# A trunk layer on one core: the columns of x for blocks 1 to 3 loaded from memory and normed there in place of transposes on TensorE, and value products that read two heads in turn

## The chip, the cores and the metric

The kernel runs on one core of a Trainium2 chip. Its time is the device time of one execution in microseconds; the figure quoted is the median of three runs. The engines that matter are PE (TensorE, matrix products), DVE (VectorE), ACT (ScalarE), POOL (GpSimd) and SP, which only issues transfers. Each runs its own instructions in order and waits on semaphores for the others.

## What is computed

One layer of a hybrid trunk over 2048 rows of 1024 columns, in float32:

```
h = _rmsnorm(x, norm1_g[layer])
proj = jnp.einsum('bsd,de->bse', h, w_in[layer])
(a_q, a_k, a_v, b_q, b_lat, i_q, i_k, i_w, gate_a, gate_b) = _split_cols(proj)
o_a = _mixer_a(...)          # sliding-window attention, 8 heads of 64, window 128, sinks
o_b = _mixer_b(...)          # indexer scores, the best 256 keys of a row, attention over them
merged = sigmoid(gate_a) * (o_a @ w_branch_a) + sigmoid(gate_b) * (o_b @ w_branch_b)
x = x + merged @ w_out
x = x + (silu(h2 @ w_ffn_gate) * (h2 @ w_ffn_up)) @ w_ffn_down     # h2 = _rmsnorm(x, norm2_g)
return _rmsnorm(x, norm_f_g)
```

Here `_rmsnorm(x, g)` is x times the inverse root of its row's mean square, times the gain g of each column. The change touches the first line (h, for three quarters of the rows) and the products of probabilities and values inside `_mixer_b`.

## The kernel before

**Tiling.** The rows are worked in four blocks of 512 (`NB`, `ROWS`). The 1024 columns lie as 8 groups of 128 (`KT`), called columns here: HT[:, k, :] holds 128 columns of h in the partitions and 512 rows along them, transposed. Products keep float32 accuracy by splitting each operand into a high part and a low remainder: `three` (L1065 to L1068) issues high x high, high x low and low x high for each column, so a job is 8 columns of three matmuls. `by_turns` makes the matmul read its 512 rows from two halves in turn, 1024 bytes apart; the result comes out in the natural order.

**Jobs.** A list (`JOBS`, L347) sets the order of the weight products: for each block b the projections iq 0 to 3 and ikw (indexer), lat (latent), and then the list `SECOND` (av, ak, aq 0 to 3, bq 0 to 3, gate 0 to 15; `s` counts in it, gate m is s = m + 10). After the projections of all four blocks follow attention, branches, output product and feed-forward, block by block. Between the columns of the SECOND jobs PE also does pieces of the indexer's scores (L1187, L1188); ACT takes their positive part (L1761) and DVE adds them up (L2337), with a MEMSET (L2342) that ends the scores of a block. In blocks 1 and 2 DVE also works at the search for the best keys of the block before (L2094 to L2131).

**Weights.** SP issues each job's weights (512 KB) into one of two buffers WRAW (L824), and behind them what `spill` adds for the job six before. POOL splits them: TENSOR_SCALAR makes WHI and TENSOR_TENSOR makes WLO (L1001, L1003), each twice per job, four columns at a time. The split of a job begins when PE has finished the job two before, since WHI and WLO have two buffers.

**The first norm and the transposes.** While block b is projected, the rows of block b + 1 lie in XN. ACT squares them at s = 11 and 12, DVE makes the mean at s = 13, ACT the root at s = 15, and DVE the inverse root SS and the scaled rows (L2056), four instructions at s = 16 to 19. PE then turns XN by multiplying with an identity (L1201): four transposes of 128x128 make one column of 128x512 in PSUM. Columns 0 to 3 of the next block are turned inside gate 15, the last job that reads the old HThi and HTlo, and columns 4 to 7 inside iq 0 of the next block. Of each turned column ACT makes HThi times the gain (L1806, `high_column`), and DVE makes HTlo as column times gain minus HThi (L2351), with the column read from PSUM. iq 0 waits for each column's HTlo (`h_split`). The gate's columns free HThi and HTlo (`h_used`).

**The value products.** In the second attention (kind "b") the transposed probabilities PThi and PTlo of two heads (128 queries each) are multiplied with the values VB: L1377 and L1379, 128x256 each, 1088 in all over the four blocks. ACT copies the sums out as XV (L1665).

## Time and profile before

| | |
|---|---|
| median of three runs | 3089.55 us (3085.45 to 3092.37) |
| profiled execution | 3089.96 us |
| its span, first to last instruction | 3087.5 us |
| PE busy | 3034.7 us (98%) |
| DVE, ACT, POOL busy | 58%, 46%, 66% |
| share of PE in the chain that ended last | 82% |
| mean granted clock of TensorE | 0.996 |

A row of a timeline gives start, duration, engine, line, instruction, output and inputs, and in brackets the idle time before it and what ended that. Matmuls overlap, so the time that one costs is the distance between two starts, not its duration. A row of a table by stretches gives, for each engine, its busy time and the number of instructions, and then the granted clock of TensorE.

### The profile page before, as it was taken

The page shows a single profiled execution, that of the slowest core. Times are in us where ns is not written, and L with a number is a line of the kernel's source. Part 1 is how long each engine was busy: PE and PEld are TensorE (multiplying, and loading weights), DVE is VectorE, ACT ScalarE, POOL GpSimd, SP SyncE. Part 2 cuts the span into 40 slices and gives each one's busy share as a digit, 9 for nine tenths or more (in the row PEclk, how much of TensorE's full clock was granted, in tenths as well). Part 3 has the DMA queues.
Part 4 walks back from the last instruction along what each step waited for, and adds up shares of the span by engine and source line. Part 5 has one row for each costly group of instructions (what it writes and reads, how often), then busy time and mean ns, then how long its engine had stood idle before and what let it go on. Part 6 is the DMA issues. An engine that isn't in the chain of part 4 may idle for free.

```text
span 3087.5 us, 44427 instructions
## 1 busy us (share of the span) xinstructions
PE 3034.7 (98%) x15678; PEld 2691.8 (87%) x15678; DVE 1805.0 (58%) x4109; ACT 1422.5 (46%) x2589; POOL 2025.0 (66%) x2201
## 2 busy tenths in 40 slices
PE   9999999999989999999999999999999999999998
PEld 8888888888888888898888888988888899888887
DVE  4336547637665555557766766967868689521111
ACT  3324545436463544347464534937655378320001
POOL 5666766665556677764777775376777922667777
PEclk9999999999999999999999999999999999999999
DMA  5766455355615333331533333163333510533333
GB/s 153 210 173 180 123 172 151 110 169 162 210 36 190 107 116 110 112 130 66 207 113 113 109 114 131 27 246 107 102 113 116 176 25 18 175 99 103 103 109 103
DMA packets 464204, 392.62 MB, mean 127 GB/s; under 512 B 29264, under 2 KB 394064, under 8 KB 463344
## 3 DMA queue, kind: packets, MB, share of 16 engines
q1 hardware_dynamic: 442544, 345.56, 37.2%
q10 hardware_dynamic: 21440, 44.22, 3.9%
q8 instruction: 126, 2.06, 0.3%
q14 instruction: 94, 0.77, 0.1%
HBM read 323.76 MB, written 62.81 MB: 125 GB/s over the span
## 4 chain that ended last, share of the span: by engine, by line
PE 82%; DVE 6%; ACT 4%; POOL 3%; issue 2%; DMA 2%; ACTq 0%; SPq 0%; DVEq 0%; POOLq 0%
PE BANK L1066 19%; PE BANK L1068 19%; PE BANK L1067 19%; PE BANK L1352 3%; PE LP L1066 3%; PE LP L1068 3%; PE LP L1067 3%; PE BANK L1377 2%; PE BANK L1379 2%; PE LP L1332 2%; PE LP L1333 2%; PE LP L1188 2%; PE LP L1187 2%; POOL WLO L1003 2%; DVE MASK L2094 1%
## 5 line engine op out<-in xcount | busy, mean ns | idle before, releaser
L1003 POOL TENSOR_TENSOR WLO<-WRAW,WHI 128x512 fp32r<-128x512 f32 x912 | 1209.3, 1326 | 76.0
L1001 POOL TENSOR_SCALAR WHI<-WRAW 128x512 fp32r<-128x512 f32 x912 | 633.3, 694 | 677.1 <-PE BANK L1068 521.8
L1066 PE MATMUL BANK<-H2hi,WHI 128*128 128x512 f32 x1376 | 524.9, 381 | 3.1 <-POOL WLO L1003 2.1
L1068 PE MATMUL BANK<-H2hi,WLO 128*128 128x512 f32 x1376 | 522.0, 379 | 0.0
L1067 PE MATMUL BANK<-H2lo,WHI 128*128 128x512 f32 x1376 | 521.9, 379 | 0.0
L1066 PE MATMUL BANK<-HThi,WHI 128*128 128x512 f32 (+1 forms) x1024 | 394.3, 385 | 1.2 <-DVE QS L2067 0.9
L1068 PE MATMUL BANK<-HThi,WLO 128*128 128x512 f32 (+1 forms) x1024 | 389.3, 380 | 0.0
L1067 PE MATMUL BANK<-HTlo,WHI 128*128 128x512 f32 (+1 forms) x1024 | 389.1, 380 | 0.0
L1773 ACT ACTIVATE MASK<-SCD,THR 128x896 bf16<-128x896 f32 (+5 forms) x186 | 282.0, 1517 | 183.2 <-DVE THR L2131 157.2
L1066 PEld LDWEIGHTS BANK<-H2hi,WHI 128*128 128x128 f32 x1376 | 260.7, 189 | 39.5 <-POOL WLO L1003 2.2
L1068 PEld LDWEIGHTS BANK<-H2hi,WLO 128*128 128x128 f32 x1376 | 260.5, 189 | 36.4
L1067 PEld LDWEIGHTS BANK<-H2lo,WHI 128*128 128x128 f32 x1376 | 260.8, 189 | 34.3
L2094 DVE TENSOR_SCALAR_CACHE_REDUCE MASK<-SCD,THR 128x640 bf16<-128x640 f32 (+2 forms) x192 | 278.1, 1486 | 3.4
L1761 ACT ACTIVATE RB<-LP 128x1024 f32<-128x1024 f32 (+7 forms) x176 | 142.6, 815 | 206.6 <-PE LP L1188 186.4
L2555 DVE TENSOR_TENSOR BANK<-BANK,SL 128x512 f32<-128x512 f32 x88 | 61.2, 695 | 297.4 <-PE BANK L1068 278.3
L2337 DVE SCALAR_TENSOR_TENSOR SCP<-RB,IW,SCP 128x1024 f32<-128x1024 f32 (+7 forms) x140 | 175.8, 1271 | 93.1 <-ACT RB L1761 91.9
L2266 DVE TENSOR_TENSOR PTlo<-BANK,PThi 128x512 fp32r<-128x512 f32 (+1 forms) x296 | 192.9, 659 | 57.1 <-ACT PThi L1702 55.1
L1068 PEld LDWEIGHTS BANK<-HThi,WLO 128*128 128x128 f32 (+1 forms) x1024 | 192.8, 188 | 28.7
L1066 PEld LDWEIGHTS BANK<-HThi,WHI 128*128 128x128 f32 (+1 forms) x1024 | 192.9, 188 | 27.6 <-DVE QS L2067 1.3
L1067 PEld LDWEIGHTS BANK<-HTlo,WHI 128*128 128x128 f32 (+1 forms) x1024 | 193.0, 188 | 25.2
L1655 ACT ACTIVATE LGb<-LGb,NMB 128x1024 f32<-128x1024 f32 (+7 forms) x192 | 174.2, 908 | 56.2 <-POOL NMB L922 52.7
L922 POOL TENSOR_SCALAR NMB<-MXB 128x1 f32<-128x1 f32 x112 | 32.3, 289 | 246.6 <-DVE MXB L2223 243.0
(314 smaller groups left out, 6445.8 us busy)
## 6 DMA issues: line engine op xcount, KB each, us to landing
WRAW<-in_w_in SPq DMA_DIRECT2D x124, 512.0 KB, 4.4
WRAW<-in_w_ffn_gate SPq DMA_DIRECT2D x88, 512.0 KB, 3.7
WRAW<-in_w_ffn_up SPq DMA_DIRECT2D x88, 512.0 KB, 3.7
WRAW<-in_w_ffn_down SPq DMA_DIRECT2D x88, 512.0 KB, 3.5
qsp<-QS SPq DMA_DIRECT2D x32, 512.0 KB, 5.8
WRAW<-in_w_out SPq DMA_DIRECT2D x32, 512.0 KB, 4.6
gates<-GS ACTq DMA_DIRECT2D x62, 256.0 KB, 2.3
GL<-gates ACTq DMA_DIRECT2D x48, 256.0 KB, 4.8
```

Source lines behind the costliest of these rows:

```text
L1001: nc.gpsimd.tensor_scalar(hi, raw, 1.0, 1.0, ALU.mult, ALU.mult).then_inc(w_hi, 1)
L1003: nc.gpsimd.tensor_tensor(lo, raw, hi.bitcast(f32), ALU.subtract).then_inc(w_split, 1)
L1066: nc.tensor.matmul(dst, whi, mhi, start=first, stop=False)
L1067: nc.tensor.matmul(dst, whi, mlo, start=False, stop=False)
L1068: return nc.tensor.matmul(dst, wlo, mhi, start=False, stop=last)
L1352: last = nc.tensor.transpose(dst[:, 2 * e + h, :], probabilities(b, kind, p, h, t), IDENT[:, :])
L1655: nc.scalar.activation(lg, lg, ACT.Exp, bias=NMB[:, slot, 0:1], accum_out=(ES if s else RS)[:, j, h0:h0 + 1]).then_inc(probs, made(probs, ...
L1761: nc.scalar.activation(RB[:, g % 2, 0:w], logits(("idx",) + key)[:, 0:w], ACT.Relu).then_inc(relu_ready, made(relu_ready, key))
L1773: nc.scalar.activation(mask_of(b)[:, j, 0:w], found_at(b, j)[:, 0:w], ACT.Sign, bias=THR[:, j:j + 1].bitcast(f32), accum_out=CNT[:, j:j + ...
L2094: last = stepped(nc.vector.tensor_scalar(junk[:, j, 0:w], found_at(b, j)[:, 0:w], threshold(j), None, op, ALU.add, accum_out=CNT[:, j:j + 1]))
L2266: nc.vector.tensor_tensor(PTLO[b][r][:, 0:w, :], trans(key)[:, 0:w, :], PTHI[b][r][:, 0:w, :].bitcast(f32), ALU.subtract).then_inc(pt_read ...
L2337: ins = nc.vector.scalar_tensor_tensor(s, r, iw, s, ALU.mult, ALU.add)
```

## The change

For blocks 1 to 3 the transposes on PE are gone. The host passes x a second time, transposed (`xt`), in the row order that `by_turns` wants. Its columns are loaded by one transfer of 2 MB into XT, which takes XN's place once the rows have been squared. The inverse roots SS (128x4) are written to memory in row order and read back broadcast to all partitions as RV (128x512). DVE multiplies each column of XT by gain and RV (L2092 of the kernel after), two columns at each of s = 21 to 24; ACT copies it to HThi; DVE subtracts (L2388). Each of the last two reads SBUF alone. The root and its reciprocal come one job earlier, and the scaling of the rows is gone. A column of HThi and HTlo is freed by gate 15's own column, for all eight. The next block's XN is loaded once HTlo is whole. Block 0 is as before.

In the second attention the value products read their probabilities in the order query, head (two heads in turn, 512 bytes apart) and not head, query; ACT puts the sums back in order as it copies XV.

```diff
+            def load_columns(b):
+                sp.wait_ge(ss_ready, n(ss_ready, (b, JT - 1)))
+                sp.dma_start(XT[:, :, :], io["xt"][:, b * ROWS:(b + 1) * ROWS].rearrange("(k p) c -> p k c", p=P)).then_inc(xt_in, 16)
+            def write_roots(b):
+                sp.wait_ge(rinv_ready, n(rinv_ready, (b, 0)))
+                sp.dma_start(io["rst"][b].rearrange("(j p) -> p j", p=P), SS[:, :], allow_slow_non_contiguous=True).then_inc(rst_moved, 16)
+            def load_roots(b):
+                sp.wait_ge(rst_moved, n(rst_moved, (b, "out")))
+                sp.wait_ge(lat_norm, n(lat_norm, b - 1))
+                sp.dma_start(RV[:, :], io["rst"][b].partition_broadcast(P)).then_inc(rst_moved, 16)
...
                 if kind == "iq" and m == 0 and b + 1 < NB:
-                    sp.wait_ge(bank_full, n(bank_full, ("xt", b, KT - 1)))
+                    if b:
+                        sp.wait_ge(h_split, n(h_split, (b, 0, KT - 1)))
+                    else:
+                        sp.wait_ge(bank_full, n(bank_full, ("xt", b, KT - 1)))
                     load_x(b + 1)
+                if kind == "gate" and b + 1 < NB:
+                    if m == 4:
+                        load_columns(b + 1)
+                    if m == 6:
+                        write_roots(b + 1)
+                    if m == 8:
+                        load_roots(b + 1)
...
-                    if used is not None and s < 4:
+                    if used is not None and s < k - 1:
...
-                        job(HThi, HTlo, (q_ready, (b, "iq", m, 1)), ready=(h_split, (b, 0)), beside=turn_more)
+                        job(HThi, HTlo, (q_ready, (b, "iq", m, 1)), ready=(h_split, (b, 0)), beside=None if b else turn_more)
...
-                        job(HThi, HTlo, release, beside=turn_next, used=(h_used, b))
+                        job(HThi, HTlo, release, used=(h_used, b))
...
-                        nc.tensor.matmul(dst, v, PTHI[b][r][:, 2 * e:2 * e + 2, :].rearrange("p h q -> p (h q)"),
+                        nc.tensor.matmul(dst, v, PTHI[b][r][:, 2 * e:2 * e + 2, :].rearrange("p h q -> p q h"),
...
-                        last = nc.tensor.matmul(dst, v, PTLO[b][r][:, 2 * e:2 * e + 2, :].rearrange("p h q -> p (h q)"),
+                        last = nc.tensor.matmul(dst, v, PTLO[b][r][:, 2 * e:2 * e + 2, :].rearrange("p h q -> p q h"),
...
+                    order = "p (g h q) -> p g h q" if kind == "a" else "p (g q h) -> p g h q"
+                    nc.scalar.copy(xv, BANK[0][:, :].rearrange(order, g=2, h=2)).then_inc(x_copied, made(x_copied, (b, kind, q)))
...
-                if b and k < 4:
-                    act.wait_ge(h_used, n(h_used, (b - 1, k)))
+                if b:
+                    if k < KT - 1:
+                        act.wait_ge(h_used, n(h_used, (b - 1, k)))
+                    else:
+                        act.wait_ge(bank_full, n(bank_full, ("gate", b - 1, 2 * KT - 1)))
+                    act.wait_ge(h_scaled, n(h_scaled, (b, k)))
+                    nc.scalar.copy(HThi[:, k, :], XT[:, k, :]).then_inc(h_hi, made(h_hi, (b, 0, k)))
+                    return
...
-                    if b + 1 < NB and s == 15:
+                    if b + 1 < NB and s == 14:
                         root_rows(b + 1)
...
-                dve.wait_ge(rinv_ready, n(rinv_ready, (b, 0)))
-                for j in range(JT):
-                    nc.vector.tensor_scalar(XN[:, j, :], XN[:, j, :], SS[:, j:j + 1], None, ALU.mult
-                                            ).then_inc(x_scaled, made(x_scaled, (b, j)))
-                    yield
+                yield
+                dve.wait_ge(xt_in, n(xt_in, b))
+                dve.wait_ge(rst_moved, n(rst_moved, (b, "in")))
+                for k in range(KT):
+                    nc.vector.scalar_tensor_tensor(XT[:, k, :], XT[:, k, :], G1[:, k:k + 1], RV[:, :], ALU.mult, ALU.mult
+                                                   ).then_inc(h_scaled, made(h_scaled, (b, k)))
+                    if k % 2:
+                        yield
...
+                    if b:
+                        nc.vector.tensor_tensor(HTlo[:, k, :], XT[:, k, :], HThi[:, k, :].bitcast(f32), ALU.subtract
+                                                ).then_inc(h_split, made(h_split, (b, 0, k)))
...
-                    if b + 1 < NB and 16 <= s <= 19:
+                    if b + 1 < NB and s in (15, 21, 22, 23, 24):
                         next(scaled)
...
+    columns = arrays["x"][0].T.reshape(arrays["x"].shape[2], -1, ROWS // 2, 2).transpose(0, 1, 3, 2)
+    arrays["xt"] = np.ascontiguousarray(columns.reshape(arrays["x"].shape[2], -1))
```

The code moves instructions on DVE and SP. On DVE, at the end of the projections of block 0, the kernel before has these rows from the reciprocal of the roots to the first query remainder of block 1 (SC is the score tile, G the gain, RB the scores' positive part):

```order
L2053 RECIPROCAL SS<-SS 128x4 [waits std_ready]
L2056 TENSOR_SCALAR XN<-XN,SS 128x1024 [waits rinv_ready]
L2056 TENSOR_SCALAR XN<-XN,SS 128x1024
L2337 SCALAR_TENSOR_TENSOR SC_104<-RB,IW,SC_104 128x512 [waits score_added,relu_ready]
L2056 TENSOR_SCALAR XN<-XN,SS 128x1024
L2337 SCALAR_TENSOR_TENSOR SC_104<-RB,IW,SC_104 128x512 [waits score_added,relu_ready]
L2056 TENSOR_SCALAR XN<-XN,SS 128x1024
L2337 SCALAR_TENSOR_TENSOR SC_104<-RB,IW,SC_104 128x512 [waits score_added,relu_ready] x4
L2342 MEMSET SC_104 64x64 [waits score_added]
L2351 SCALAR_TENSOR_TENSOR HTlo<-LP,G_72,HThi 128x512 [waits h_hi] x8
L2067 SCALAR_TENSOR_TENSOR Q<-BANK,Q 64x512 [waits q_hi,bank_full]
```

The same place of the kernel after:

```order
L2087 RECIPROCAL SS<-SS 128x4 [waits std_ready]
L2374 SCALAR_TENSOR_TENSOR SC_105<-RB,IW,SC_105 128x512 [waits score_added,relu_ready] x5
L2092 SCALAR_TENSOR_TENSOR XT<-XT,G_72,RV 128x512 [waits rst_moved,xt_in]
L2092 SCALAR_TENSOR_TENSOR XT<-XT,G_72,RV 128x512
L2374 SCALAR_TENSOR_TENSOR SC_105<-RB,IW,SC_105 128x512 [waits score_added,relu_ready]
L2092 SCALAR_TENSOR_TENSOR XT<-XT,G_72,RV 128x512 x2
L2374 SCALAR_TENSOR_TENSOR SC_105<-RB,IW,SC_105 128x512 [waits score_added,relu_ready]
L2379 MEMSET SC_105 64x64 [waits score_added]
L2092 SCALAR_TENSOR_TENSOR XT<-XT,G_72,RV 128x512 x4
L2388 TENSOR_TENSOR HTlo<-XT,HThi 128x512 [waits h_hi] x8
L2104 SCALAR_TENSOR_TENSOR Q<-BANK,Q 64x512 [waits q_hi,bank_full]
```

The row scalings ahead of the scores are gone, four column scalings stand among the last scores, and four more between the MEMSET and the eight rows of HTlo.

At the end of the projections of block 1, DVE in the kernel before ends the scores and does two steps of the search (TAKE, THR, MASK) ahead of HTlo:

```order
L2342 MEMSET SCP 64x64 [waits score_added]
L2121 TENSOR_SCALAR TAKE<-CNT 128x1 [waits topk_step]
L2125 TENSOR_SCALAR TAKE<-CNT 128x1 [waits tiles_counted]
L2131 TENSOR_SCALAR THR<-TAKE,THR 128x1 [waits topk_step] x2
L2094 TENSOR_SCALAR MASK_124,CNT<-SC_104,THR 128x384 [waits threshold_set]
...
L2351 SCALAR_TENSOR_TENSOR HTlo<-LP,G_72,HThi 128x512 [waits h_hi] x8
```

The same place of the kernel after:

```order
L2379 MEMSET SCP 64x64 [waits score_added]
L2092 SCALAR_TENSOR_TENSOR XT<-XT,G_72,RV 128x512 x2
L2158 TENSOR_SCALAR TAKE<-CNT 128x1 [waits topk_step]
L2162 TENSOR_SCALAR TAKE<-CNT 128x1 [waits tiles_counted]
L2168 TENSOR_SCALAR THR<-TAKE,THR 128x1 [waits topk_step] x2
L2131 TENSOR_SCALAR MASK_125,CNT<-SC_105,THR 128x384 [waits threshold_set]
L2092 SCALAR_TENSOR_TENSOR XT<-XT,G_72,RV 128x512 x2
...
L2388 TENSOR_TENSOR HTlo<-XT,HThi 128x512 [waits h_hi] x8
```

Four column scalings stand two by two ahead of the two steps of the search; the second step, left out here, is like the first. At the end of block 2 the order is that of block 0.

On SP's queue the kernel after has these rows in the projections of block 0 (WRAW are the weights, of gate 10 in the fourth row; ft are tables of the relative bias):

```order
L855 DMA WRAW_52<-in_w_in 128x8x128 [waits w_split]
L603 DMA XT<-in_xt 128x8x512 [waits ss_ready]
L633 DMA ft<-FT_134 8x16x384
L855 DMA WRAW_51<-in_w_in 128x8x128 [waits w_split]
L633 DMA ft<-FT_134 8x16x384
L855 DMA WRAW_52<-in_w_in 128x8x128 [waits w_split]
L609 DMA rst<-SS 128x4x1 [waits rinv_ready]
...
L855 DMA WRAW_52<-in_w_in 128x8x128 [waits w_split]
L616 DMA RV<-rst 128x512 [waits lat_norm,rst_moved]
```

The three new transfers stand between weight loads, two loads apart from each other.

## Rows read from the trace of the kernel before

**Rows 1.** The page: busy time of PE, and the chain that ended last.

```profile
PE 3034.7 (98%) x15678; PEld 2691.8 (87%) x15678; DVE 1805.0 (58%) x4109; ACT 1422.5 (46%) x2589; POOL 2025.0 (66%) x2201
PE BANK L1066 19%; PE BANK L1068 19%; PE BANK L1067 19%; PE BANK L1352 3%; PE LP L1066 3%; PE LP L1068 3%; PE LP L1067 3%; PE BANK L1377 2%; PE BANK L1379 2%; PE LP L1332 2%; PE LP L1333 2%; PE LP L1188 2%; PE LP L1187 2%; POOL WLO L1003 2%; DVE MASK L2094 1%
```

**Rows 2.** Timeline of PE in gate 15 of block 2: start, us, engine, line, instruction.

```profile
606.89 0.38 PE L1066 MATMUL BANK<-HThi,WHI 128*128 128x512 f32 x1
...
607.54 0.38 PE L1066 MATMUL BANK<-HThi,WHI 128*128 128x512 f32 x1
...
608.19 0.60 PE L1201 MATMUL LP<-IDENT,XN 128*128 128x128 f32 x4
...
609.28 0.49 PE L1201 MATMUL LP<-IDENT,XN 128*128 128x128 f32 x3
```

**Rows 3.** Table by stretches: gate 15's start to iq 1's start, three changes.

```profile
190.50:204.37 13.87, 13.87 (x82) 12.23 (x80) 7.57 (x10) 7.07 (x11) 7.85 (x8) 1.00 0.67 167
387.61:401.48 13.87, 13.87 (x81) 12.22 (x80) 9.35 (x22) 9.16 (x17) 8.05 (x8) 1.00 0.43 124
601.25:615.13 13.88, 13.88 (x82) 12.22 (x81) 7.92 (x11) 7.07 (x11) 8.57 (x8) 1.00 0.47 131
```

**Rows 4.** Timeline of DVE there: end of the scores, and HTlo after the search.

```profile
192.99 0.11 DVE L2342 MEMSET SC<- 64x64 f32 x1
...
390.29 0.11 DVE L2342 MEMSET SCP<- 64x64 f32 x1
...
393.20 2.73 DVE L2351 SCALAR_TENSOR_TENSOR HTlo<-LP,G,HThi 128x512 fp32r<-128x512 f32 x4
...
603.22 0.11 DVE L2342 MEMSET SCP<- 64x64 f32 x1
```

**Rows 5.** Timeline of POOL at the third change: splits of iq 0 and iq 1.

```profile
602.69 1.59 POOL L1003 TENSOR_TENSOR WLO<-WRAW,WHI 128x512 fp32r<-128x512 f32 x1
604.26 0.61 POOL L1001 TENSOR_SCALAR WHI<-WRAW 128x512 fp32r<-128x512 f32 x1
604.95 1.28 POOL L1003 TENSOR_TENSOR WLO<-WRAW,WHI 128x512 fp32r<-128x512 f32 x1
608.52 0.62 POOL L1001 TENSOR_SCALAR WHI<-WRAW 128x512 fp32r<-128x512 f32 x1 [2.29 <-PE BANK L1068]
```

**Rows 6.** All of two lines: ns shortest/median/longest, first and last start in us.

```profile
L2393 DVE TENSOR_TENSOR AKSlo<-KAT,AKShi x16: 682/838/1404, 65.3 to 659.0; 64x512 fp32r<-64x512 f32 x16
...
L2351 DVE SCALAR_TENSOR_TENSOR HTlo<-LP,G,HThi x32: 742/751/753, 14.7 to 612.8; 128x512 fp32r<-128x512 f32 x32
```

**Rows 7.** Timelines of DVE and of POOL, one moment of block 0.

```profile
65.31 1.39 DVE L2393 TENSOR_TENSOR AKSlo<-KAT,AKShi 64x512 fp32r<-64x512 f32 x1 [3.21 <-ACT AKShi L1846]
...
64.89 1.27 POOL L1003 TENSOR_TENSOR WLO<-WRAW,WHI 128x512 fp32r<-128x512 f32 x1
```

**Rows 8.** Table by stretches around an idle time of PE: clock behind POOL's time.

```profile
679.50:682.80 3.30, 1.42 (x8) 1.25 (x8) 2.34 (x4) 2.57 (x5) 0.00 (x0) 1.00 0.94 231
682.90:686.10 3.20, 3.20 (x10) 2.63 (x9) 1.43 (x2) 0.91 (x2) 1.18 (x2) 0.50 0.17 68
```

**Rows 9.** Timelines of PE, products of 256 columns, and groups by line and form.

```profile
2561.56 0.28 PE L1377 MATMUL BANK<-PThi,VB 128*128 128x256 f32 x1
...
2561.91 0.28 PE L1379 MATMUL BANK<-PTlo,VB 128*128 128x256 f32 x1
...
1009.14 0.28 PE L1520 MATMUL BANK<-H2hi,WHI 128*128 128x256 f32 x1
...
1009.36 0.28 PE L1522 MATMUL BANK<-H2hi,WLO 128*128 128x256 f32 x1
...
L1379 PE MATMUL BANK<-PTlo,VB 128*128 128x256 f32 x544 | 141.9, 282 | 0.0
...
L1521 PE MATMUL BANK<-H2lo,WHI 128*128 128x256 f32 x64 | 17.6, 275 | 0.0
```

**Rows 10.** Table by stretches: the load of XN for block 1.

```profile
30.00:52.00 22.00, 22.00 (x104) 18.18 (x103) 5.99 (x12) 6.03 (x11) 14.88 (x18) 1.00 0.58 174
```

More of the change, by code:

```diff
@@ L133, in trunk_program @@
         XN = at("XN", [P, JT, D], f32, rX + 16384)
+        XT = at("XT", [P, KT, ROWS], f32, rX + 16384)
         SC0 = at("SC0", [P, TK, ROWS], f32, rX + 32768)
@@ L228, in trunk_program @@
         var_ready, std_ready, rinv_ready = sem("var_ready"), sem("std_ready"), sem("rinv_ready")
-        h_ready, h_hi, h_split, h_used = sem("h_ready"), sem("h_hi"), sem("h_split"), sem("h_used")
+        h_hi, h_split, h_used = sem("h_hi"), sem("h_split"), sem("h_used")
         q_hi, q_ready = sem("q_hi"), sem("q_ready")
@@ L232, in trunk_program @@
         lat_ready, lat_norm, lat_hi, lat_split = sem("lat_ready"), sem("lat_norm"), sem("lat_hi"), sem("lat_split")
-        v_hi, v_ready, vat_ready, carried = sem("v_hi"), sem("v_ready"), sem("vat_ready"), sem("carried")
+        v_hi, v_ready, vat_ready = sem("v_hi"), sem("v_ready"), sem("vat_ready")
         kat_ready = sem("kat_ready")
@@ L251, in trunk_program @@
         pt_hi, pt_ready = sem("pt_hi"), sem("pt_ready")
-        o_step, o_ready, ot_ready = sem("o_step"), sem("o_ready"), sem("ot_ready")
+        o_ready, ot_ready = sem("o_ready"), sem("ot_ready")
         o_added, o_scaled = sem("o_added"), sem("o_scaled")
@@ L262, in trunk_program @@
         g_ready, first_ready, last_ready = sem("g_ready"), sem("first_ready"), sem("last_ready")
+        xt_in, rst_moved, h_scaled = sem("xt_in"), sem("rst_moved"), sem("h_scaled")
         near_in, near_v = sem("near_in"), [sem(f"near_v{i}") for i in range(2)]
@@ L595, in load_x @@
                     sp.dma_start(XN[:, j, :], x[0, first:first + 2 * P - 1:2, :]).then_inc(x_in[j], 16)
+            def load_columns(b):
+                sp.wait_ge(ss_ready, n(ss_ready, (b, JT - 1)))
+                made(xt_in, b, 16)
+                sp.dma_start(XT[:, :, :], io["xt"][:, b * ROWS:(b + 1) * ROWS].rearrange("(k p) c -> p k c", p=P)).then_inc(xt_in, 16)
+            def write_roots(b):
+                sp.wait_ge(rinv_ready, n(rinv_ready, (b, 0)))
+                made(rst_moved, (b, "out"), 16)
+                sp.dma_start(io["rst"][b].rearrange("(j p) -> p j", p=P), SS[:, :], allow_slow_non_contiguous=True).then_inc(rst_moved, 16)
+            def load_roots(b):
+                sp.wait_ge(rst_moved, n(rst_moved, (b, "out")))
+                sp.wait_ge(lat_norm, n(lat_norm, b - 1))
+                made(rst_moved, (b, "in"), 16)
+                sp.dma_start(RV[:, :], io["rst"][b].partition_broadcast(P)).then_inc(rst_moved, 16)
             def load_constants():
@@ L1227, in turn_more @@
                         turn_rows(b, s + 4)
-                def turn_next(s):
-                    if 2 <= s < 6:
-                        turn_rows(b + 1, s - 2)
                 if b == 0:
@@ L1664, in x_copy @@
                         act.wait_ge(trans_full, n(trans_full, ("x", b) + quads(b)[quads(b).index((kind, q)) - 2]))
-                    nc.scalar.copy(XVS[b][q % 2][:, :, :].rearrange("p h q -> p (h q)"), BANK[0][:, :]
-                                   ).then_inc(x_copied, made(x_copied, (b, kind, q)))
+                    xv = XVS[b][q % 2][:, :, :].rearrange("p (g h) q -> p g h q", h=2)
+                    order = "p (g h q) -> p g h q" if kind == "a" else "p (g q h) -> p g h q"
+                    nc.scalar.copy(xv, BANK[0][:, :].rearrange(order, g=2, h=2)).then_inc(x_copied, made(x_copied, (b, kind, q)))
                 def out_copy(kind, j):
@@ L2348, in project @@
                 for k in range(KT):
-                    bk = bank(("xt", b, k))
                     dve.wait_ge(h_hi, n(h_hi, (b, 0, k)))
-                    nc.vector.scalar_tensor_tensor(HTlo[:, k, :], bk[:, :], G1[:, k:k + 1], HThi[:, k, :].bitcast(f32),
-                                                   ALU.mult, ALU.subtract).then_inc(h_split, made(h_split, (b, 0, k)))
+                    if b:
+                        nc.vector.tensor_tensor(HTlo[:, k, :], XT[:, k, :], HThi[:, k, :].bitcast(f32), ALU.subtract
+                                                ).then_inc(h_split, made(h_split, (b, 0, k)))
+                    else:
+                        nc.vector.scalar_tensor_tensor(HTlo[:, k, :], bank(("xt", b, k))[:, :], G1[:, k:k + 1], HThi[:, k, :].bitcast(f32),
+                                                       ALU.mult, ALU.subtract).then_inc(h_split, made(h_split, (b, 0, k)))
                 if b == 0:
@@ L2639, in build @@
     io["rsd"] = nc.dram_tensor("rsd", (blocks, JT, HEADS, P), f32).ap()
+    io["rst"] = nc.dram_tensor("rst", (blocks, ROWS), f32).ap()
     io["scd"] = nc.dram_tensor("scd", (blocks, JT, P, seq), f32).ap()
```

## The prediction

> **What bounds the kernel now.** I read the page's busy times and chain first. PE is busy 98% of the span and carries 82% of the chain [rows 1]: a microsecond of PE work taken away is gained if nothing else is late there, and a microsecond of new waiting on PE is lost in full. So the edits are costed by what PE executes and by when its operands are ready. The timeline of PE around the end of a block's projections gives the price of a column and of a group of transposes [rows 2]; the table by stretches shows the three block changes, each without an idle moment of PE [rows 3]; the timelines of DVE and POOL there show what those two do meanwhile [rows 4, 5].
>
> I count from the start of gate 15, the last job of a block that reads HThi and HTlo, to the start of iq 1, the second job of the next block. Between them lie 16 columns (eight of gate 15, eight of iq 0) and eight groups of four transposes: 13.87, 13.87 and 13.88 us [rows 3].
>
> **The transposes.** One column (three matmuls of 512) starts 0.65 us after the one before (606.89 to 607.54); a column with four transposes ahead takes 1.09 us (608.19 to 609.28) [rows 2]. A group costs 0.44 us. 24 groups go (eight for each of three blocks): 24 x 0.44 = **-10.5 us** of PE work, 3.5 us at each change, whose 16 columns then need 13.87 - 3.5 = 10.35 us.
>
> **What takes their place.** Before, HTlo of a column was one DVE instruction with one SBUF operand (the other was PSUM). After, a column is scaled on DVE by gain and inverse root (two SBUF tensors), copied by ACT, and subtracted on DVE (two SBUF tensors). By the order, four of the eight scalings and all eight subtractions stand behind the MEMSET that ends the scores, at every change; at the second one also two steps of the search. These twelve instructions run while gate 15 and iq 0 run, and iq 0 needs their results, the last one 0.65 us before iq 1 can start.
>
> DVE is free of the MEMSET at 193.10, 390.40 and 603.33 [rows 4], which is 2.6, 2.8 and 2.1 us after gate 15's start [rows 3]. A two-SBUF subtraction takes 0.68 us at least [rows 6]; with its start I take 0.70, so twelve are 8.4 us. The two search steps are what lies between 390.40 and 393.20: 2.8 us [rows 4].
>
> Then POOL. The same subtraction took 1.39 us at 65.31, where a TENSOR_TENSOR of POOL (1.27 us) had begun at 64.89 [rows 7]: it ended 0.54 us after POOL's did, so it stood still for some 0.7. Over its 16 the spread is 0.68 to 1.40 with a median of 0.84, where the PSUM form keeps to 0.74 to 0.75 over 32 [rows 6]. That is the reason why this matters only after the change. POOL's split of iq 1 begins when gate 15 is done, as at 608.52 [rows 5]; without transposes that is 8 x 0.65 = 5.2 us after gate 15's start, in the middle of the twelve. Two TENSOR_SCALAR of 0.62 and two TENSOR_TENSOR of 1.28 then stand among them, beside what is left of iq 0's split (602.69 to 606.23 at the third change [rows 5]). For each POOL instruction that comes between two of DVE's I charge 1.1 us for a TENSOR_TENSOR (between the 0.7 of [rows 7], where it was a third over, and its full 1.28) and 0.4 for a TENSOR_SCALAR (between 0 and 0.62; no row shows one alone against a two-SBUF instruction).
>
> The Trainium skill, "SBUF — State Buffer", section "Who interferes with whom", says that a DVE instruction with two SBUF inputs contends with a GpSimd one that reads SBUF, while one with at most one SBUF input doesn't, and that the shared ports are held for a whole instruction. The trace agrees in the sizes just given (1.39 against 0.68, and 0.74 to 0.75 throughout); that a back-to-back row of DVE instructions alternates with POOL's no row shows. By clean instructions the three changes would cost -3.4 us net, by the median of the 16 (12 x 0.84 for 12 x 0.70 each time) +1.6, by turns +7.9.
>
> - First change: 2.6 + 0.3 to start + 8.4 + three TENSOR_TENSOR and two TENSOR_SCALAR (4.1) = 15.4; the last column makes 16.05, which is 2.2 later than 13.87.
> - Second: 2.8 + 0.3 + 8.4 + 2.8 of search + 1.9 (one TENSOR_TENSOR and two TENSOR_SCALAR; the rest falls into the search, which does without the second SBUF tensor) = 16.2; 16.85, 3.0 later.
> - Third: 2.1 + 0.9 (the TENSOR_TENSOR begun at 602.69 runs until 604.28) + 8.4 + three of each (4.5) = 15.9; 16.55, 2.7 later.
>
> Sum **+7.9 us** net: 10.5 saved, 18.4 of new waiting on PE. Without POOL's share it is 11.95, 14.75 and 11.45, so -1.9 + 0.9 - 2.4 = -3.4; with every POOL instruction at full length +10.7. I take the alternation, since both engines have work queued all the while.
>
> **The clock.** PE was busy 1.42 of 3.30 us in 679.50 to 682.80, and the next 3.20 us ran at 0.50 of its clock [rows 8], the lower of the two levels (1.2 GHz), which costs 1.6 us of work. After the change PE waits some 6 us at each block change, in pieces between columns. None to two such stretches may follow a change, partly while PE waits anyway: 0 to +9.6 us, taken **+2.3** (half of one each).
>
> **The value products.** 1088 matmuls of 256 columns, 544 on each of two lines that the chain names [rows 1, 9], start 0.117 us apart (2561.56 to 2561.91, three of them) with their probabilities read one after another. Products of 256 columns that read rows in turn, 1024 bytes apart, start 0.110 apart (1009.14 to 1009.36, two) [rows 9]. The mean lengths, 282 and 275 ns, say the same 7 ns [rows 9]: 1088 x 0.007 = 7.6 us. After, the two heads lie 512 bytes apart, a distance that no row shows: 0 to -8.7 (8 ns, where the starts are rounded that way). Both lines are on the chain, so it counts in full; I take **-7.5**. ACT's reordering copy of the result moves the same elements; taken as 0.
>
> The Trainium skill, "SBUF — State Buffer", in the section "Door 1: The DMA port swizzle", speaks against this edit: SBUF lines are 16 bytes, and each access that crosses to a new line pays. Reading heads in turn would then touch a new line at every element. The two rows at 1024 bytes say the reverse for TensorE (0.110 against 0.117); by the rule the term is 0 or above, by the rows -7.5.
>
> **Costed at nothing.** The 2 MB of x in columns comes on SP's queue between gate weights. The like load of XN stands ahead of weights too, and PE was busy 22.00 of 22 us across it [rows 10]; if that cover fails, 0 to 2 us a block. The roots go out two weight loads ahead of the load that brings them back, and by its place ahead of gate 14's weights that one goes out during gate 10, a job ahead of the scaling that waits for it; if late, the scores queued behind it on DVE wait, and PE's score matmuls with them. XN's scaling leaves DVE at a place where it isn't late. The first four scalings replace it there.
>
> **Sum.** 3089.96 (profiled execution) + 7.9 + 2.3 - 7.5 = 3092.7. The median stands 0.4 below the profiled one: **3092 us**. About 0.2%, 6 us, is what a measurement of this kernel can tell from no change: 3083.4 to 3095.7.
>
> **Rivals.**
> - *Forecast*, chance 0.50: 3092, from 3086 to 3098. The subtractions take turns with POOL and eat the transposes' gain; the values pay.
> - *DVE is in time*, 0.20: POOL loses the turns or its instructions fall beside ACT's copies, net -3.4 to 0 at the changes, no slow clock: 3089.96 - 0.4 - 1.7 - 7.5 = 3080, from 3075 to 3084. For it: the median of [rows 6] is nearer to the clean value. Against: POOL's split sits exactly among the twelve [rows 5].
> - *The values in turn gain nothing*, 0.18, the part that then doesn't do what it says: 3092.3 + 7.5 = 3100. For it: no row at 512 bytes. Against: the pair at 1024 [rows 9]. The rule of the Trainium skill on 16-byte lines (same page, "SBUF — State Buffer") is on its side and would give this time or a later one; the chance goes by the rows.
> - *Slower through the clock*, 0.12: at the block changes the stretches at 0.50 are two each instead of a half, 9.6 instead of 2.3 us: 3099.6. [...]
>
> Faster by over 0.2%: the second, 0.20, and an edge of the first, 0.21. Slower: the third and fourth less their edges, and the upper edge of the first: 0.15 + 0.10 + 0.09 = 0.34. Within: 0.45. The range is 3080 to 3103: it leaves out half of the second case and the ends of the last two.
>
> **What the profile after would show.** No transposes outside block 0. Gate 15 eight columns long (5.2 us), then iq 0 with idle before its columns, released by HTlo's subtraction, together about 18 us over three changes; subtractions with a median well over 0.68 and pieces of 1.3 to 2 us beside POOL's splits; iq 1 starting 16 to 17 us after gate 15. Value products 111 ns apart and 275 ns long. I am wrong in the second term if iq 1 starts at 12 to 14; in the values if they stay at 119; in the covered edits if PE waits for weights (WLO) in gates 10 to 14 or DVE for the roots.

## The result, and the profile after

| | median | lowest to highest | runs |
|---|---|---|---|
| before | 3088.99 us | 3085.45 to 3092.37 | 4 |
| after | 3104.58 us | 3102.18 to 3108.47 | 4 |

The ratio is 1.0052 (95% interval 1.0034 to 1.0069): the kernel became some 16 us slower. The forecast was 3092 us, no change that can be measured, from 3080 to 3103; the time lies just above that range. The profiled execution of after took 3108.47 us with a span of 3106.7, which is 19.2 us more than the span of before; it is the slowest of the four, 3.9 us above their median.

The busy times on the page of after (busy us, share of the span, instructions) answer to [rows 1]:

```profile
PE 3026.4 (97%) x15582; PEld 2677.5 (86%) x15582; DVE 1822.7 (59%) x4121; ACT 1419.4 (46%) x2589; POOL 2027.4 (65%) x2201
```

PE has 96 instructions and 8.3 us less to do, and yet the end came 19.2 us later: PE stands idle 27.5 us longer. The page doesn't say where; the waits of PE do (who waited for whom, us in total, times, longest):

```profile
PE BANK L1097 <- DVE HTlo L2388: 14.6, 4, 6.2
PE BANK L1097 <- POOL WLO L1034: 8.9, 4, 6.8
```

The first is the wait that the prediction spoke of, at the block changes. The second, for weights, has one piece of 6.8 us that it had costed at nothing. The table by stretches places both: gate 10 to gate 12 of block 0, and gate 15 to iq 1 at the three changes, which answer to [rows 3] (stretch, length, busy time of PE, its weight loads, DVE, ACT and POOL with instructions, granted clock, share and rate of the DMA):

```profile
163.03:184.32 21.29, 14.49 (x53) 11.91 (x52) 1.63 (x2) 2.28 (x4) 8.80 (x10) 0.76 0.74 125
201.16:218.08 16.92, 13.64 (x50) 10.95 (x49) 13.21 (x14) 6.04 (x11) 9.35 (x8) 0.80 0.64 161
401.55:420.39 18.84, 12.66 (x49) 10.51 (x48) 15.18 (x27) 8.47 (x17) 10.28 (x8) 0.82 0.42 113
621.74:640.72 18.98, 13.81 (x49) 11.04 (x48) 14.76 (x15) 6.23 (x12) 10.38 (x8) 0.82 0.38 105
```

Gate 10 to gate 12 took 11.2 us in before, and so 10.1 us more here:

```profile
162.44:173.66 11.22, 11.22 (x53) 9.85 (x52) 5.11 (x4) 2.17 (x4) 9.02 (x9) 1.00 0.69 179
```

The changes are 3.0, 5.0 and 5.1 us longer than the 13.87 to 13.88 of before. In all four the clock fell, from 1.00 to 0.76 and 0.80 to 0.82. The four stages of the value products, from the first start to the last of each, gave 5.8 us back (383.3 against 389.1 us). 10.1 + 13.1 - 5.8 is 17.4 of the 19.2 us; the rest is spread in pieces of a microsecond.

These sizes are those of one execution. In the profile of columns_alone (below), whose projections are the same, the stretch from gate 10 to gate 12 is 9.4 us longer than in before and the three changes together 9.9. And 1.6 of the 5.8 us aren't the products': in before the granted clock was 0.50 from 908.2 to 911.4 us, in stage one, which took 42.2 us there and 40.6 in two kernels with the old products and no such stretch in it (reads_first_alone and pieces_in_before, below).

**At a block change.** DVE and POOL at the third one (timelines: start, us, engine, line, instruction; a row with x4 or x8 is a run of instructions), which answer to [rows 4, 5]:

```profile
625.09 0.11 DVE L2379 MEMSET SCP<- 64x64 f32 x1
625.13 5.28 DVE L2092 SCALAR_TENSOR_TENSOR XT<-XT,G,RV 128x512 f32<-128x512 f32 x4
630.32 6.38 DVE L2388 TENSOR_TENSOR HTlo<-XT,HThi 128x512 fp32r<-128x512 f32 x8
```

```profile
625.58 1.58 POOL L1034 TENSOR_TENSOR WLO<-WRAW,WHI 128x512 fp32r<-128x512 f32 x1
627.25 0.94 POOL L1032 TENSOR_SCALAR WHI<-WRAW 128x512 fp32r<-128x512 f32 x1
628.27 1.58 POOL L1034 TENSOR_TENSOR WLO<-WRAW,WHI 128x512 fp32r<-128x512 f32 x1
629.82 1.05 POOL L1032 TENSOR_SCALAR WHI<-WRAW 128x512 fp32r<-128x512 f32 x1
630.96 1.58 POOL L1034 TENSOR_TENSOR WLO<-WRAW,WHI 128x512 fp32r<-128x512 f32 x1
```

Twelve DVE instructions took 11.57 us (625.13 to 636.70). While POOL worked, four scalings took 5.28 us, 1.32 each, and two subtractions 2.70 (630.32 to 633.02). POOL's last row ends at 632.54, and the six subtractions behind it took 3.69 us; at the second change, where POOL's last row ended at 412.17, all eight took 4.90:

```profile
633.02 3.69 DVE L2388 TENSOR_TENSOR HTlo<-XT,HThi 128x512 fp32r<-128x512 f32 x6
...
412.24 4.90 DVE L2388 TENSOR_TENSOR HTlo<-XT,HThi 128x512 fp32r<-128x512 f32 x8
```

POOL's rows were longer too: 1.58 and 1.05 where 1.28 and 0.62 stand in [rows 5]. PE then ran iq 0 at half clock, as the stretch that answers to [rows 8] shows (clock behind POOL's time):

```profile
632.40:639.10 6.70, 6.01 (x15) 4.78 (x15) 4.31 (x7) 0.00 (x0) 0.14 (x1) 0.50 0.31 81
```

The last subtraction ended at 636.70, and iq 1 started at 640.72, not 0.65 us behind it: PE was still working off columns at 1.28 us each.

**In block 0.** SP's queue around the write of the roots, the split of gate 11's weights on POOL, and PE ahead of gate 11:

```profile
156.52 0.38 SPq L855 DMA_DIRECT2D WRAW<-in_w_in  x1
156.95 3.62 SPq L609 DMA_DIRECT2D rst<-SS  x1
...
164.28 0.38 SPq L855 DMA_DIRECT2D WRAW<-in_w_in  x1
164.71 6.50 SPq L633 DMA_DIRECT2D ft<-FT  x1
177.42 0.38 SPq L855 DMA_DIRECT2D WRAW<-in_w_in  x1
```

```profile
173.50 0.62 POOL L1032 TENSOR_SCALAR WHI<-WRAW 128x512 fp32r<-128x512 f32 x1 [9.24 <-DMA WRAW<-in_w_in]
```

```profile
175.60 0.76 PE L1097 MATMUL BANK<-HThi,WHI 128*128 128x512 f32 x1 [6.80 <-POOL WLO L1034]
```

The weights of gate 11 went out at 156.52, 0.4 us ahead of the roots, and POOL could begin on them only at 173.50; those of gate 12 went out at 164.28 and those of gate 13 only 13 us later. The transfers of 156 to 172 us, by kind (count, KB each, median us to landing):

```profile
WRAW<-in_w_in SPq DMA_DIRECT2D x2, 512.0 KB, 15.5
gates<-GS ACTq DMA_DIRECT2D x3, 256.0 KB, 12.8
ft<-FT SPq DMA_DIRECT2D x2, 192.0 KB
rst<-SS SPq DMA_DIRECT2D x1, 2.0 KB, 18.8
```

In before, from 155.9 to 172 us:

```profile
WRAW<-in_w_in SPq DMA_DIRECT2D x3, 512.0 KB, 4.3
gates<-GS ACTq DMA_DIRECT2D x3, 256.0 KB, 4.5
```

The smallest transfer, 2 KB of roots in 512 pieces of 4 bytes, took longest, ACT's gates on another queue were late as well, and so were gate 11's weights, which had been issued ahead of it (16.9 us).

**The value products** answer to [rows 9] (groups by line and form: busy us, mean ns, idle before; and a timeline):

```profile
L1406 PE MATMUL BANK<-PTlo,VB 128*128 128x256 f32 x544 | 136.5, 276 | 0.0
```

```profile
2587.95 0.27 PE L1404 MATMUL BANK<-PThi,VB 128*128 128x256 f32 x1
...
2588.28 0.28 PE L1406 MATMUL BANK<-PTlo,VB 128*128 128x256 f32 x1
```

276 ns long instead of 282, and 0.110 us from start to start (2587.95 to 2588.28, three), as the rows at 1024 bytes had said.

### The profile page after: what moved, and what is told of

Same layout as the page of the kernel before. It is cut to its first block, busy times and chain, and to the rows that moved or that the text cites. A ratio compares the mean times of both kernels' runs of the same rounds, so it can differ in the third digit from the quotient of the medians.

```text
span 3106.7 us, 44253 instructions
## 1 busy us (share of the span) xinstructions
PE 3026.4 (97%) x15582; PEld 2677.5 (86%) x15582; DVE 1822.7 (59%) x4121; ACT 1419.4 (46%) x2589; POOL 2027.4 (65%) x2201
## 4 chain that ended last, share of the span: by engine, by line
PE 80%; DVE 8%; ACT 4%; POOL 3%; issue 2%; DMA 2%; ACTq 0%; SPq 0%; DVEq 0%; POOLq 0%
PE BANK L1097 19%; PE BANK L1098 19%; PE BANK L1099 19%; PE BANK L1379 3%; PE LP L1097 3%; PE LP L1099 3%; PE LP L1098 3%; PE BANK L1404 2%; PE LP L1359 2%; PE LP L1218 2%; PE LP L1219 2%; PE LP L1360 2%; POOL WLO L1034 2%; PE BANK L1406 2%; DVE MASK L2131 1%
```

## The experiments

Each kernel was measured beside before on one chip; ratios are to before, with the 95% interval.

**Which part loses.** `values_alone` is before with the second part alone, whose edit this is; `columns_alone` is after with it undone:

```diff
-                        nc.tensor.matmul(dst, v, PTHI[b][r][:, 2 * e:2 * e + 2, :].rearrange("p h q -> p (h q)"),
+                        nc.tensor.matmul(dst, v, PTHI[b][r][:, 2 * e:2 * e + 2, :].rearrange("p h q -> p q h"),
...
```

PTLO and the copy of XV go with it.

> The kernel before with the value products in turn and the reordering copy, nothing else. Theory (the part does what it says, 512 bytes apart as at 1024): 7.6 us less, ratio 0.9975, products 275 ns long instead of 282. Rival (two heads 512 bytes apart gain nothing): ratio 1.000, length still 282.

> The kernel after with the value products as before. Theory (the parts add up): the loss of 15.6 us is 7.6 gained by the values and some 23 lost by the columns, so ratio 1.0075: 10 us between gate 10 and gate 12 of block 0, 13 us at the three block changes. Rival (the values lost too, or the parts hinder each other): ratio 1.005 or less.

Measured: columns_alone 1.0072 (1.0059 to 1.0084), 3109.63 us, as the theory had it; values_alone 1.0001 (0.9992 to 1.0009), as the rival had it, although its products were 276 ns long. Its profile shows where the gain went. Stage three, 111.70 us in before, was 118.90 us, and a single wait stands in it. SP, POOL and PE there (timelines), and of all 24 read-backs RR the time from issue to landing (us, shortest, median and longest):

```profile
1963.91 1.70 SPq L757 DMA_DIRECT2D RR<-rsd  x2
1966.09 0.37 SPq L746 DMA_DIRECT2D rsd<-RS  x1
```

```profile
1974.58 0.72 POOL L941 TENSOR_TENSOR OTB<-XZ,RR 128x256 f32<-128x256 f32 x1 [7.43 <-DMA RR<-rsd]
```

```profile
1977.85 0.58 PE L1377 MATMUL BANK<-PThi,VB 128*128 128x256 f32 x1 [5.90 <-ACT XV L1667]
```

```profile
DMA to landing us min/median/max: 2.6/2.7/9.9
```

The sums of the softmax (RS) go to memory 4 bytes a piece and come back broadcast as RR. With faster products the next write left 0.5 us after the two reads had been issued (until 1965.61, then 1966.09), and the second of them landed after 9.9 us. POOL waited for it with the next maximum (NMB) behind in its queue, and ACT, DVE and PE behind that: PE waited 5.9 us, and behind that its granted clock was 0.50 (1976.1 to 1982.8). In before the same write left at 1969.01, as the second read landed (1969.02):

```profile
1965.44 1.53 SPq L757 DMA_DIRECT2D RR<-rsd  x2
1969.01 0.37 SPq L746 DMA_DIRECT2D rsd<-RS  x1
```

That could have been chance, so the kernel was run again, and then with one wait more:

> The kernel of values_alone once more, since its profiled execution held a wait of 5.9 us that no other one shows (a read-back of the sums that took 9.9 us). Theory (that wait is chance, the products are worth 6 us in the attention): ratio 0.998, the four stages of the value products 382 us together and not 389. Rival (the products' gain is lost again each time, in the hand-over of the sums): ratio 1.000 and stages of 386 or more.

Measured: 0.9996 (0.9985 to 1.0006), and again a read-back of 8.0 us at the same place. The rival holds.

```diff
             def hand_sums(b, q):
+                if q:
+                    sp.wait_ge(sum_in[(q - 1) % 2], n(sum_in[(q - 1) % 2], (b, q - 1)))
```

> The kernel of values_alone with one wait more on SP: the sums of a group of heads are written (4 bytes a piece) only when the read-back of the group before has landed. Theory (in both profiles of values_alone the write went out 1.5 us behind a read at 1965 and held it up to 8.0 and 9.9 us instead of 2.7, which gave the gain back): no read-back over 4 us, the four stages 382 to 383 us, ratio 0.998. Rival (the lost gain lies elsewhere): ratio 1.000.

> The kernel before with only the wait on SP: the sums of a group are written when the read-back of the group before has landed. Theory (the products in turn bring the gain, the wait only keeps it): in the kernel before the write goes out behind the landed read anyway (1969.01 against 1969.02), so ratio 1.000. Rival (the wait itself is the gain): ratio 0.9985.

> The kernel of values_reads_first once more, on the chip of reads_first_alone. Theory: ratio 0.9985 again, 4 to 6 us below reads_first_alone. Rival: no difference between the two.

Measured: values_reads_first 0.9985 (0.9976 to 0.9994), again 0.9980 (0.9971 to 0.9989), 3084.60 and 3083.83 us; reads_first_alone 0.9998 (0.9989 to 1.0007), 3088.76 us. So by the medians the products are worth some 5 us, the wait alone nothing, and the gain is kept only with the wait. In values_reads_first no read-back takes over 4.0 us:

```profile
DMA to landing us min/median/max: 2.6/2.7/4.0
```

The four stages took 383.8 and 383.1 us there, 387.5 in reads_first_alone.

**The stall in block 0.** `root_write_dropped` is after without the write of block 1's roots; RV of block 1 is read from a row of x in their place:

```diff
-                    if m == 6:
+                    if m == 6 and b:
                         write_roots(b + 1)
```

> The kernel after, but the roots of block 1 aren't written to memory; RV of block 1 takes a row of x in their place, so block 1's projections are computed from wrong roots. Theory (the 512 pieces of 4 bytes hold up the weights queued behind them): gate 11 of block 0 starts 5.6 us after gate 10 again and not 12.6, and some 10 us come back: ratio 1.002. Rival (the 2 MB of columns and the table writes fill the queues by themselves): gate 11 is as late as before, ratio 1.005.

Measured: 1.0041 (1.0026 to 1.0057), 3099.54 us against the 3104.58 of after; the stall is gone (gate 10 to gate 12):

```profile
162.62:173.85 11.23, 11.23 (x54) 9.83 (x53) 1.50 (x2) 2.17 (x4) 7.78 (x9) 1.00 0.78 207
```

10 us came back in this stretch, 5 in the medians, where the two intervals overlap. A part of the difference stands in the stages of the value products, which took 387.6 us in this profile and 383.3 in that of after; why is open.

`tables_earlier` is after with the table writes at other jobs:

```diff
-                if 22 <= i < 38:
-                    write_table(i - 22)
+                if 8 <= i < 24:
+                    write_table(i - 8)
```

> The kernel after with the sixteen table writes of block 0 fourteen jobs earlier, clear of the columns and the roots. Theory (the table writes and the 4-byte pieces together hold up the weights; blocks 1 and 2 have the pieces without table writes and no stall): gate 11 is on time, some 10 us come back, ratio 1.002. Rival (the pieces alone do it): the roots still take 18 us to land and gate 11 is late, ratio 1.005.

Measured: 1.0072 (1.0059 to 1.0086). The stall shrank from 6.8 to 3.7 us, and 3.7 us of new waiting came at 90.5, where the tables now collide with other transfers (weights issued from 77 to 94 us land after 7.1 to 8.7 us, in after 4.6 to 5.5). Nothing gained; the tables are a part of the stall, but not all of it: without them the roots still took 13.6 us to land.

`pieces_in_before` is before with the write of the roots added on SP, and a wait for it two jobs later:

```diff
+                if kind == "gate" and m == 6 and b + 1 < NB:
+                    sp.wait_ge(rinv_ready, n(rinv_ready, (b + 1, 0)))
+                    sp.dma_start(io["rst"][b + 1].rearrange("(j p) -> p j", p=P), SS[:, :], allow_slow_non_contiguous=True).then_inc(rst_moved, 16)
```

> The kernel before, which also writes the inverse roots of blocks 1 to 3 (128x4, 4 bytes a piece) to memory with gate 6's spill, as the kernel after does; nobody reads them. Theory (the pieces alone hold up what is queued behind them): the write takes 10 to 19 us to land, gate 11 or 12 of block 0 is some 3 to 7 us late and a stretch at half clock follows, ratio 1.001 to 1.003. Rival (it takes the 2 MB of columns ahead of them): no wait, ratio 1.000.

Measured: 1.0005 (0.9996 to 1.0015), the rival's. The pieces do hold up what is queued with them, as the transfers of 158 to 170 us in this kernel show:

```profile
WRAW<-in_w_in SPq DMA_DIRECT2D x2, 512.0 KB, 9.9
gates<-GS ACTq DMA_DIRECT2D x2, 256.0 KB, 9.8
...
rst<-SS SPq DMA_DIRECT2D x1, 2.0 KB, 10.9
```

But weights that land in 9.9 us and not in 4.3 are almost in time for PE: gate 11 starts 6.1 us after gate 10 and not 5.6. The pieces are needed for the stall (without them it is gone) and don't make it alone; it takes other load beside them. In after these are the tables and the 2 MB of columns (with the columns but not the tables 3.7 us of the stall were left, with the tables but not the columns 0.5), behind which the weights of gate 10 had already taken 9.6 us to land.

**The wait at the changes.** `clock_filler` is after, with something to do for PE while it waits for the first HTlo:

```diff
+                        if s == 0 and ready[1][0]:
+                            for _ in range((0, 14, 27, 20)[ready[1][0]]):
+                                nc.tensor.matmul(dst[:, :], KIhi[:, 0:P], KIhi[:, 0:ROWS], start=True, stop=True)
                         pe.wait_ge(ready[0], n(ready[0], (*ready[1], s)))
```

> The kernel after, with 14, 27 and 20 products of 512 columns (some 0.215 us each) that nobody reads on PE ahead of iq 0 of blocks 1, 2 and 3, in the time in which PE waits for the first HTlo. Theory (the stretches at half clock cost 2.1, 2.1 and 3.4 us at the three changes): no stretch at 0.50 there, iq 1 starts 14.8, 16.7 and 15.6 us after gate 15 and not 16.9, 18.8 and 19.0; 7.6 us less, ratio 1.003. Rival (the subtractions alone set when iq 1 starts): 16.9 to 19.0 stays, ratio 1.005.

Measured: 1.0039 (1.0023 to 1.0054), 3101.99 us. The three changes, with work that nobody reads in them:

```profile
199.42:214.67 15.25, 14.35 (x64) 11.37 (x62) 13.26 (x14) 6.05 (x11) 9.39 (x8) 1.00 0.69 176
398.29:415.05 16.76, 16.76 (x76) 14.03 (x75) 15.22 (x27) 8.49 (x17) 10.36 (x8) 1.00 0.46 126
616.67:632.76 16.09, 15.33 (x70) 12.62 (x68) 14.80 (x15) 6.26 (x12) 10.43 (x8) 1.00 0.44 122
```

Clock 1.00 throughout, and 48.1 us in place of 54.7: PE does more and is done 6.6 us sooner. The theory holds, a little short of its 7.6. Against other executions it is less: in columns_alone, root_write_dropped and tables_earlier, whose code there is that of after, the changes took 51.5 to 52.9 us. In the medians the gain isn't clear of noise (the intervals of 1.0039 and of after's 1.0052 overlap).

`scalings_earlier` takes the four scalings among the twelve instructions away from there, by a norm that is six jobs earlier in all its steps (the last of them is shown):

```diff
-                    if b + 1 < NB and s in (15, 21, 22, 23, 24):
+                    if b + 1 < NB and s in (9, 17, 18, 19, 20):
                         next(scaled)
```

> The kernel after with the norm's steps six jobs earlier (squares at s = 5 and 6, columns loaded with bq 0's spill, roots written with bq 2's and read with gate 1's, scalings at s = 17 to 20), so that only the eight subtractions stand behind the MEMSET, and the roots' write lies ahead of the table writes. Theory (the twelve instructions make the wait, and the roots' pieces beside the tables the stall in block 0): iq 1 starts 12.6 to 14.5 us after gate 15, gate 11 is on time; 13 and 10 us less, 3082 us, ratio 0.998. Rival (POOL's turns and the clock make the wait whatever the number of DVE's instructions): iq 1 at 15.5 or later, ratio 1.001 or more.

Measured: 1.0030 (1.0018 to 1.0042), 3100.45 us. At the changes the theory held in full, 40.1 us and clock 1.00, below the 41.6 of before:

```profile
201.80:214.38 12.58, 11.14 (x50) 8.79 (x49) 10.42 (x10) 6.05 (x11) 9.31 (x8) 1.00 0.67 166
400.95:415.31 14.36, 11.64 (x49) 8.67 (x48) 11.68 (x22) 8.48 (x17) 9.60 (x8) 1.00 0.47 134
618.40:631.54 13.14, 11.40 (x50) 8.66 (x49) 11.82 (x11) 6.05 (x11) 10.80 (x8) 1.00 0.44 123
```

In the stall it failed. The roots' write, clear of the tables and of the columns (those had landed at 114, it left at 121.3), now had 512 KB of spilled queries behind it (122.3), and PE waited again, 7.0 us in one piece:

```profile
PE BANK L1097 <- POOL WLO L1034: 11.8, 5, 7.0
```

In the medians the gain over after (1.0030 against 1.0052) isn't clear of noise either.

**Mended versions.** In `all_mended` RV doesn't go through memory: PE turns the roots, ACT copies them.

```diff
+                    if s == 11 and b + 1 < NB:
+                        pe.wait_ge(rinv_ready, n(rinv_ready, (b + 1, 0)))
+                        dst = take("bank", rst_moved, b + 1, ("rv", b + 1))
+                        for j in range(JT):
+                            last = nc.tensor.transpose(dst[:, j * P:(j + 1) * P], SS[:, j:j + 1].to_broadcast([P, P]), IDENT[:, :])
+                        last.then_inc(bank_full, made(bank_full, ("rv", b + 1)))
```

> The kernel of scalings_earlier with RV made on PE (four transposes of the roots spread over 128 columns) and copied by ACT, so that no roots go through memory, and with the write of the sums behind the read-back. Theory (all that the change lost is the stall by 4-byte pieces, the twelve instructions and the clock that they pulled down): no wait of PE for WLO in gates 8 to 12, changes of 12.6, 14.3 and 13.1 us, the values' 6 us kept: 3082 us, ratio 0.998. Rival (the columns' 2 MB or the scalings among the scores cost as much as the transposes did): ratio 1.000 or more.

> The kernel of all_mended without the values' part and without the wait ahead of the sums: the columns' part alone, mended. Theory (8 DVE instructions behind the MEMSET and no pieces of roots): 1.6 us less at the changes, 1.4 more for the roots on PE, 2 to 3 more where the scalings lengthen the scores of block 2: ratio 1.0000 to 1.0010. Rival (without the stall the part pays): ratio 0.998 or less.

Measured: all_mended 1.0013 (1.0004 to 1.0022), columns_roots_on_pe 1.0028 (1.0016 to 1.0039), later than the theory in both, though the block changes (40.1 us) and gates 10 and 11 (11.2 us) are as it had them. A new wait stands in the feed-forward, in both kernels:

```profile
PE BANK L1538 <- DVE X L2534: 5.6, 2, 3.0
```

The roots take a result bank three times, which turns the ring of four banks by three for all that follows. `all_mended_aligned` skips one place more:

```diff
+                if b == NB - 1:
+                    taken["bank"] += 1
```

> The kernel of all_mended with one place more skipped in PE's ring of four result banks ahead of block 3, since the three takes for the roots had turned the ring by three and two matmul groups of the feed-forward (L1538) then waited 5.6 us for DVE's sums in a bank that before was free. Theory (that wait and its clock are the larger part of what all_mended has over values_reads_first): no wait for X ahead of L1538, 5 us less, 3086 us, ratio 0.999. Rival (the columns themselves cost it): 3091 us, ratio 1.001.

Measured: 0.9994 (0.9985 to 1.0003), 3087.27 us, and that wait is gone. Mended in all places, the change as a whole is even with before; values_reads_first, which leaves the columns' part out, is the fastest kernel of the study, at 3083.83 to 3084.60 us. What the columns' part still costs stands mostly in block 2 as far as the profiles show: from its iq 1 to its gate 15 the three kernels with the roots on PE took 203.0 to 205.6 us, before and values_reads_first 199.8 to 201.0. No run takes that apart.

## Why the prediction was wrong

| term, us | forecast | measured in the profile of after |
|---|---|---|
| DVE's instructions against the transposes, clock apart | +7.9 | +5.5 |
| half clock at the changes | +2.3 | +7.6 |
| covered edits (columns, roots, XN) | 0 | +10.1 in block 0 |
| value products | -7.5 | -5.8 |
| sum | +2.7 | +17.4 |

The right column is one execution, the slowest of the four of after. In columns_alone the first two rows make +9.9 and the third +9.4; of the -5.8 the products made some 4.2 (387.5 to 383.3 us), and the rest is the slow stretch in stage one of before.

- **The transposes.** -10.5 us of PE work is right: 24 groups are gone.
- **What takes their place.** The step held, and came to somewhat less than forecast. With PE at full clock iq 1 would start (an estimate) 0.65 us behind the last subtraction, or 5.2 us behind iq 0's start: 14.8, 16.7 and 15.6 us after gate 15, against 16.05, 16.85 and 16.55 in the prediction. The clean instruction was priced too high: 8.4 us for twelve at 0.70, where eight subtractions took 4.90 and four scalings at their shortest, 0.74, make 3.0, together 7.9 (an estimate). So some 3.7 of the 11.57 us at the third change are turns with POOL, not 4.5, while the first scaling started 3.4 us after gate 15 and not 3.0. The turns fell on the scalings more than on the subtractions, whose median stayed clean where the prediction looked for one well over 0.68; the rows below answer to [rows 6]. (One slip beside the sum: the second change without POOL's share is 14.95, not 14.75, and the net then -3.2, not -3.4.) The Trainium skill, "SBUF — State Buffer", section "Who interferes with whom", says that a DVE instruction with two SBUF inputs contends with a GpSimd one that reads SBUF. The rows at 625 to 637 us agree (two subtractions in 2.70 us beside POOL, six in 3.69 behind it). No run took POOL away, so the turns are read from the trace, not shown by an experiment.

```profile
L2092 DVE SCALAR_TENSOR_TENSOR XT<-XT,G,RV x24: 737/1101/1771, 192.3 to 628.6; 128x512 f32<-128x512 f32 x24
...
L2388 DVE TENSOR_TENSOR HTlo<-XT,HThi x24: 676/686/1755, 207.9 to 636.0; 128x512 fp32r<-128x512 f32 x24
```

- **The clock.** The mechanism was named and even stood as the rival of the slower side; its size was wrong. Half a stretch of 3.2 us was taken for each change (three halves at 1.6 us are 2.4, not 2.3), and in this execution each change got some 6.7 us at 0.50. The prediction had PE wait in pieces between columns; by the order the first subtraction comes only behind all scalings, so PE waits 3.3, 6.2 and 4.5 us in one piece before the first column. clock_filler shows 6.6 us, the trace 7.6.
- **Costed at nothing.** This step failed, and the sign that the prediction had named for it is there, a wait for WLO ahead of gate 11. The cover was checked with the load of XN [rows 10], 2 MB with nothing behind it but weights. In after the 2 MB are followed at once by a write in 4-byte pieces and by table writes, and the sum of these used up the weights' lead and 6.8 us more; half clock behind it made 10.1. The bound, 0 to 2 us a block, names no row. The write's own duration had not been priced at all.
- **The value products.** Right in kind, 276 ns and 0.110 us at 512 bytes. The Trainium skill, "SBUF — State Buffer", section "Door 1: The DMA port swizzle", says that each access that crosses to a new 16-byte line pays, and here every element is on a new line. The rows say cheaper (0.110 us from start to start for 0.117), so the rule doesn't hold for these reads of PE. Not all of it was on the path (the four stages lost some 4.2 us, not 7.5), and alone it is given back by the collision above. In the profile of after no read-back was long.
- **The rivals** were set up as one or another. The time came from two at once, a wait at the changes with its clock, for which a rival had 7.3 us more, and a delayed load, which had 0 to 2 us a block and no chance of its own; the range was right for either and too narrow for both.

## What to carry to other kernels

Price a transfer by what is in flight with it, issued behind it or just ahead, and a scattered one by its pieces: here 2 KB in 4-byte pieces cost 0.6 us in before and 10 us behind a 2 MB load, and a faster stage slid such a write against a read and lost its gain until an order was forced. When work moves from PE to an engine that PE then waits for, count the clock beside the wait; put such work where the waiting engine isn't late (four scalings moved earlier gave 14.7 us at the changes against the profile of after, 11.4 against that of columns_alone). After adding a user to a ring of buffers, check that the ring stands as before for what follows.

## What the runs showed of the hardware that was not expected

- A write of 512 pieces of 4 bytes took 9.8 to 18.8 us to land in after and 10.9 when added to before, where 512 KB loads on its own queue then took 9.9 us instead of 4.3 and stores from ACT's 9.8 instead of 4.5 (15.5 and 12.8 in after). A load issued 0.4 us ahead of it was held up like those behind (10.1 us in before, 16.9 in after).
- A read of 64 KB whose issue ended 0.5 us ahead of such a write landed after 9.9 us instead of 2.7, although it was issued first; with the write held back until the read had landed, none took over 4.0.
- Matmuls without use kept the granted clock at 1.00 where waiting had let it fall to 0.50, and the three stretches took 48.1 us, where four executions without them took 51.5 to 54.7.
- DVE and POOL rows side by side were both longer: 1.32 for 0.74 us and 1.58 for 1.28.
